# Modulation vectors of a two-layer transformer kernel: summed by VectorE among the projections, or multiplied by TensorE in the attention

## The reference

```python
def layer(x, ctx, c, c_ctx, w_mod, b_mod, ...):
    shift, scale, gate = jnp.split(jax.nn.silu(c) @ w_mod + b_mod, 3, axis=-1)
    shift_c, scale_c, gate_c = jnp.split(jax.nn.silu(c_ctx) @ w_mod + b_mod, 3, axis=-1)
    hx = rmsnorm(x, g_pre) * (1 + scale[:, None]) + shift[:, None]
    hc = rmsnorm(ctx, g_pre) * (1 + scale_c) + shift_c
    # projections q, k, v, ga, uf, gf, zc, bc, cc, gc = hx @ w_in (and the same of hc in layer 0)
    # window attention over own and context keys, a Fourier mix, a short convolution, a gated merge with w_out
    x_new = x + gate[:, None] * rmsnorm(y, g_post)
    ctx = ctx + gate_c * rmsnorm(yc, g_post)      # layer 0 only
```

## Time and profile before

| | us |
|---|---|
| median of 3 runs | 2080.86 |
| lowest, highest | 2075.86, 2082.39 |
| the profiled execution, whole | 2084.84 |
| its span (first to last instruction) | 2083.0 |
| first block, about | 760 |
| attention of layer 0, layer 1 | 132.5, 82 |
| projections of layer 0 after q1, layer 1 after q1 | 159, 110 |

### The profile page before, as it was taken

One profiled execution on the slowest core, in us unless ns is written; L12 is line 12 of the kernel. 1 busy time (PEld: TensorE's weight loads), 2 busy tenths in 40 slices (PEclk: granted clock), 3 DMA queues, 4 the chain that ended last, 5 costly groups with the idle time before them and its releaser, 6 DMA issues.

```text
span 2083.0 us, 27285 instructions
## 1 busy us (share of the span) xinstructions
PE 2012.9 (97%) x10646; PEld 1670.8 (80%) x10646; DVE 704.9 (34%) x1701; ACT 859.2 (41%) x1620; POOL 777.1 (37%) x616
## 2 busy tenths in 40 slices
PE   8999999999999999989999999999998999999997
PEld 4888888877888978867888888888877788888885
DVE  3121355343325445177431111017337551111004
ACT  3221377446237546477332222114557623222211
POOL 1433355315444134310344444434430144444442
PEclk9999989999999999999999999999989999999999
DMA  9521133221223123300233333222420123333320
GB/s 272 160 89 61 57 98 121 81 51 61 89 94 102 38 78 120 119 21 1 81 102 87 96 101 103 100 94 82 122 87 11 42 81 101 84 99 101 115 88 41
DMA packets 206310, 183.74 MB, mean 88 GB/s; under 512 B 31686, under 2 KB 182588, under 8 KB 206184
## 3 DMA queue, kind: packets, MB, share of 16 engines
q1 hardware_dynamic: 200152, 170.67, 27.2%
q10 hardware_dynamic: 6032, 11.33, 1.6%
HBM read 179.86 MB, written 5.40 MB: 89 GB/s over the span
## 4 chain that ended last, share of the span: by engine, by line
PE 85%; DVE 6%; ACT 4%; POOL 2%; issue 2%; DMA 0%; ACTq 0%; SPq 0%; DVEq 0%
PE ps L1263 22%; PE ps L1265 22%; PE ps L1264 22%; PE ps L1363 3%; PE ps L1856 3%; PE ps L1871 3%; POOL w_lo L691 2%; PE ps L1882 2%; PE ps L1337 2%; PE ps L1349 2%; PE ps L1301 1%; PE ps L1394 1%; ACT w_hi L745 1%; DVE sc L2429 1%; DVE sc L2441 1%
## 5 line engine op out<-in xcount | busy, mean ns | idle before, releaser
L691 POOL TENSOR_TENSOR w_lo<-raw,w_hi 128x512 fp32r<-128x512 f32 x582 | 755.2, 1329 | 1201.2 <-ACT w_hi L745 1201.1
L745 ACT ACTIVATE w_hi<-raw 128x1024 fp32r<-128x1024 f32 (+2 forms) x293 | 291.5, 1037 | 246.7 <-PE ps L1265 244.4
L1263 PE MATMUL ps<-g_hi,w_lo 128*128 128x512 f32 (+1 forms) x928 | 352.7, 380 | 1.6 <-POOL w_lo L691 1.6
L1264 PE MATMUL ps<-g_lo,w_hi 128*128 128x512 f32 (+1 forms) x928 | 351.8, 379 | 0.0
L1265 PE MATMUL ps<-g_hi,w_hi 128*128 128x512 f32 (+1 forms) x928 | 351.8, 379 | 0.0
L1263 PEld LDWEIGHTS ps<-g_hi,w_lo 128*128 128x128 f32 x928 | 174.6, 188 | 38.2 <-issue 1.3
L1265 PEld LDWEIGHTS ps<-g_hi,w_hi 128*128 128x128 f32 x928 | 174.6, 188 | 35.9
L1264 PEld LDWEIGHTS ps<-g_lo,w_hi 128*128 128x128 f32 x928 | 174.6, 188 | 35.2
L1263 PE MATMUL ps<-h_hi,w_lo 128*128 128x512 f32 (+1 forms) x496 | 181.0, 365 | 2.0 <-POOL w_lo L691 1.2
L1264 PE MATMUL ps<-h_lo,w_hi 128*128 128x512 f32 (+1 forms) x496 | 175.9, 355 | 0.0
L1265 PE MATMUL ps<-h_hi,w_hi 128*128 128x512 f32 (+1 forms) x496 | 175.8, 354 | 0.0
(11 more groups left out here) (282 smaller groups left out, 3451.0 us busy)
## 6 DMA issues: line engine op xcount, KB each, us to landing
raw<-in_w_in SPq DMA_DIRECT2D x30, 1024.0 KB, 5.3
raw<-in_w_mod SPq DMA_DIRECT2D x24, 1024.0 KB, 5.3
raw<-in_w_gate SPq DMA_DIRECT2D x44, 512.0 KB, 3.9
raw<-in_w_up SPq DMA_DIRECT2D x44, 512.0 KB, 5.2
raw<-in_w_down SPq DMA_DIRECT2D x22, 1024.0 KB, 4.8
raw<-in_w_out SPq DMA_DIRECT2D x8, 1024.0 KB, 5.1
strips<-bias_rows ACTq DMA_DIRECT2D x18, 256.0 KB, 4.1
raw<-in_w_in SPq DMA_DIRECT2D x16, 256.0 KB, 4.5
```

What stands on the lines that cost most here:

```text
L691: pool.tensor_tensor(w_lo[:, i % SPLIT, a:e], raw_of(what)[:, a:e], w_hi[:, i % SPLIT, a:e].bitcast(F32), ALU.subtract).then_inc(s_tile_lo ...
L745: act.activation(w_hi[:, i % SPLIT, a:b], raw_of(what)[:, a:b], ACT.Copy).then_inc(s_tile_hi.sem, s_tile_hi.nth((what, n)))
L1263: pe.matmul(o, lhs[1], rhs[0], start=first, stop=False)
L1264: pe.matmul(o, lhs[0], rhs[1], start=False, stop=False)
```

## The change

The sixteen tiles of `w_mod` are no longer split nor given to TensorE as moving data. They are cut into eight blocks of 512 columns (`BLOCKS`), each in two tiles of 4 x 128 rows (`WEIGHED`), and loaded among the projection tiles (`GOES_BEFORE`): two before kv, two before uf, one each before gf, zc, bc, two before cc, one before gc and two before ga0 in layer 0; one each before uf, gf, zc and cc in layer 1. VectorE's `weigh` multiplies each 128 x 512 piece of the raw tile by the condition value of its partition and adds it up in `acc` (float32, in SBUF), for both condition vectors: eight operations a tile, 128 in all. SyncE's load of a tile three places behind such a tile waits for its weigh. TensorE's `add_up` then sums the partitions of a block: eight matmuls with 128x128 pieces of `acc` as the stationary part and one column of ones, placed in a projection's PSUM bank before its part 1 (layer 0) or ahead of a projection (layer 1). VectorE's `summed_in` adds the bias. `mod`, `mod_fm`, `mod_out_row`, `mods_out` and `cond_hl` are gone, and so are the splits in the attention. The constants' and `w_fourier`'s loads now stand ahead of the first weighed tile instead of kv. The freed bank 7 gives the attention a second output bank (`slots`).

```diff
@@ stream
+        BLOCKS = [(0, 4), (0, 5), (1, 0), (1, 1), (1, 2), (1, 3), (1, 4), (1, 5)]
+        WEIGHED = [(l, "mod", jb, kh) for l, jb in BLOCKS for kh in range(2)]
+        GOES_BEFORE = {(0, "kv"): (0, 1), (0, "uf"): (2, 3), (0, "gf"): (4,), (0, "zc"): (5,), (0, "bc"): (6,), (0, "cc"): (7, 8),
+                       (0, "gc"): (9,), (0, "ga", 0): (10, 11), (1, "uf"): (12,), (1, "gf"): (13,), (1, "zc"): (14,), (1, "cc"): (15,)}
+        SUMMED = {(0, "kv", 1): 0, (0, "gf", 0): 1, (0, "zc", 0): 2, (0, "bc", 1): 3, (0, "gc", 0): 4, (0, "ga", 0, 1): 5,
+                  (1, "zc", 0): 6, (1, "ga", 0, 0): 7}
-            stream += mix + [mod_tile(*m) for m in mods_in_attention[l]] + outs
+            for tile in mix:
+                for m in GOES_BEFORE.get(tile[0], ()):
+                    wl, _, jb, kh = WEIGHED[m]
+                    stream.append((WEIGHED[m], [square(I["w_mod"][wl], jb, kh)], False))
+                stream.append(tile)
+            stream += outs
-        MOD_STEP = (4, 6)
-            return sc, pt, 1024, (2, 1, 1, 4)
+            return sc, pt, 1024, (2, 1, 2, 4)
@@ sync
+                    elif stream[n - RAW][0] in WEIGHED:
+                        sp.wait_ge(s_weigh.sem, s_weigh.at(stream[n - RAW][0]))
@@ scalar
+                    if j == 1:
+                        act.wait_ge(s_mod.sem, s_mod.at(("sum", 5 + 2 * l)))
-                    if step >= 4 and (step - 4) % MOD_STEP[l] == 0 and mods:
-                        mod_out_row(mods.pop(0))
-                        split_next((0,))
-                        halves.append(step)
-                    elif halves and step == halves[-1] + 2:
-                        halves.pop()
-                        split_next((1,))
@@ tensor
+            def add_up(n, b):
+                pe.wait_ge(s_weigh.sem, s_weigh.at(WEIGHED[2 * n + 1]))
+                for h in range(2):
+                    for c in range(4):
+                        o = 256 + 2 * c + h
+                        m = pe.matmul(ps[:, b, o:o + 1], acc[n % 2][h][:, P * c:P * c + P], ones[:, 0:1], start=True, stop=True)
+                m.then_inc(s_mod.sem, s_mod.nth(("sum", n)))
+                emptied[b] = s_mod_in.after(("sum", n))
-                        if before:
-                            mod_fm(before.pop())
-                        mod(what)
-                        before.append(what)
@@ vector
+            def weigh(m):
+                what, n, kh = WEIGHED[m], m // 2, m % 2
...
+                wait_landed(dve, what)
+                for k in range(4):
+                    for h in range(2):
+                        to, w = acc[n % 2][h], raw_of(what)[:, 512 * k:512 * k + 512]
+                        by = cond[:, 4 * kh + k, h:h + 1]
+                        if kh == 0 and k == 0:
+                            V.tensor_scalar(to[:], w, by, None, ALU.mult).then_inc(s_weigh.sem, s_weigh.nth((what, k, h)))
+                        else:
+                            dve.wait_ge(s_weigh.sem, s_weigh.at((what, k - 1, h) if k else (WEIGHED[m - 1], 3, h)))
+                            V.scalar_tensor_tensor(to[:], w, by, to[:], ALU.mult, ALU.add).then_inc(s_weigh.sem, s_weigh.nth((what, k, h)))
```

More of the change, by code:

```diff
@@ L220, in _program @@
         ao1 = at("ao1", [P, NT, 512], uf_at)
+        acc_at = names["ga"][0] + 2 * 4 * TOK
+        acc = [[at("acc00", [P, 512], acc_at), at("acc01", [P, 512], acc_at + 2048)],
+               [at("acc10", [P, 512], acc_at + 4096), at("acc11", [P, 512], names["mod_row"][0])]]
+        assert names["mod_row"][1] == 2048 and 6144 <= 2 * 4 * TOK
         tmp_m = at("tmp_m", [P, 2, 512], names["q1"][0])
@@ L472, in _program @@
         assert all(split_at[(DEPTH + l, "up")] % SPLIT == UP_SLOT for l in range(DEPTH))
-        mods_all = FIRST + [what for what, _, _ in stream if what[1] == "mod" and what not in FIRST]
-        mod_at = {what: i for i, what in enumerate(mods_all)}
         ROW_BANK = (4, 5, 6, 7, 2, 4, 5, 2)
@@ L969, in _ @@
                     split_next()
-                mods = [(m, "mod", j) for m, j in mods_in_attention[l]]
                 n_q = len(units1(l)) // HEADS
-                halves = []
                 def between(step):
@@ L1289, in paired @@
                 return [(0, 0), (1, 0), (0, 1), (1, 1), (2, 0), (3, 0), (2, 1), (3, 1)]
-            def mod(what):
-                i = mod_at[what]
-                o = ps[0:4, 7, 0:256]
-                w = both_parts(begin(what), lambda r: r.rearrange("p (k c) -> p k c", k=KD))
-                if i >= 1:
-                    pe.wait_ge(s_mod_row.sem, s_mod_row.at(mods_all[i - 1]))
-                for part in range(2):
-                    for k in range(KD):
-                        need(what, 256 * (k + 1))
-                        m = pe.matmul(o, cond_hl[:, k, :], w[1 - part][:, k, :], start=part == 0 and k == 0, stop=part == 1 and k == KD - 1)
-                m.then_inc(s_mm.sem, s_mm.nth(what))
-                left(what)
-            def mod_fm(what):
-                i = mod_at[what]
-                l, _, j = what
-                pe.wait_ge(s_mod_row.sem, s_mod_row.at(what))
-                for c in range(2):
-                    o = 256 + 64 * l + 2 * (2 * j + c)
-                    m = pe.matmul(ps[:, 7, o:o + 2], mod_row[0:4, i % 2, P * c:P * c + P], fold[0:4, :], start=True, stop=True)
-                m.then_inc(s_mod.sem, s_mod.nth(what))
+            def add_up(n, b):
[6 more added lines that the diff above has]
+                emptied[b] = s_mod_in.after(("sum", n))
             def attend(y, units, at_step):
@@ L1365, in attend @@
                     at_step(step)
-                for b in range(7):
+                for b in range(8):
                     if 512 * b < width * n_s:
@@ L1513, in fm @@
                         emptied[b] = until.after((l, what, c, part))
+                        if part == 1 and (l, *what, c) in SUMMED:
+                            add_up(SUMMED[l, *what, c], b)
                         for k in range(KD):
@@ L1589, in _ @@
                             n_rot += 1
+                        if l == 1 and (l, what, c) in SUMMED:
+                            pe.wait_ge(*emptied[4])
+                            add_up(SUMMED[l, what, c], 4)
                         fm((what,), c, w, s_conv_t if what == "cc" else s_proj)
@@ L1594, in _ @@
                     for c in range(2):
+                        if l == 1 and (l, "ga", j, c) in SUMMED:
+                            pe.wait_ge(*emptied[5])
+                            add_up(SUMMED[l, "ga", j, c], 5)
                         fm(("ga", j), c, w, s_proj)
@@ L1637, in _ @@
                 units = units1(l)
-                mods = [(m, "mod", j) for m, j in mods_in_attention[l]]
-                before = []
                 def between(step):
@@ L1643, in between @@
                         fourier(step)
-                    if step >= 3 and (step - 3) % MOD_STEP[l] == 0 and mods:
-                        if step == 3:
-                            pe.wait_ge(*emptied[7])
-                        what = mods.pop(0)
-                        if before:
-                            mod_fm(before.pop())
-                        mod(what)
-                        before.append(what)
-                attend(l, units, between)
-                while mods:
-                    what = mods.pop(0)
-                    mod_fm(before.pop())
-                    mod(what)
-                    before.append(what)
-                mod_fm(before.pop())
-                emptied[7] = s_mod_out.after((l, 1))
+                attend(l, units, between)
                 pe.wait_ge(s_lo.sem, s_lo.at((l, "s", SIDES[3])))
@@ L2170, in _ @@
                 if l == 0:
+                    weigh(0)
+                    weigh(1)
                     dve.wait_ge(s_consts.sem, 16 * len(consts))
@@ L2221, in _ @@
                 q_lo(1)
+                summed_in((5, 7)[l])
                 def k_lo_part(g):
```

91 lines of the change are left out of this document (58 added, 33 removed).

## The result

The changed kernel took 2028.6 us (median of 4 runs, 2018.2 to 2029.1) beside 2081.6 before (4 runs, 2075.9 to 2093.6): ratio 0.973, interval 0.967 to 0.978. The forecast was 2060 with a range of 2043 to 2079: the sign was right, and the gain of 53 us was two and a half times the 20.5 forecast. The profiled execution has a span of 2027.3 us (before 2083.0).

The account below looks back on a forecast made before the run. TensorE, busy 97% of the span, was taken as the bound. Gains 36.1 + 2.6 + 1 less costs 15.2 (add_up) and 4 (queue order) gave 20.5 us off the 2080.86 median: 2060 us, range 2043 to 2079.

Parts of the forecast that it names:

- cond_hl and the two mods_out go: Small removed VectorE and ScalarE work of 0.2 to 0.4 us beside a busy TensorE, forecast to gain nothing.
- rival C: Half-clock stretch in layer 0's attention is a chance event: 2052 if it stays away, 2068 if a second comes; chance 0.12.
- The matmuls: Removing the attentions' modulation tiles from TensorE: 2.37 us a tile at full clock, 36.1 us gained in all.
- ScalarE's share: Removing mod_row copies and splits ahead of attention's copies: +6.6 us of waits, net 2.6 after a charge of 4.
- the heads' ends: Charge in layer 0's attention for half-width context units: 0.5 us for each of eight heads, -4 us.
- The second bank: Second attention output bank lets a product start earlier: about 1 us in layer 0, 0.5 in layer 1; gain 1 booked.
- the first tile is no gain: Each attention's first modulation tile: TensorE waits for ScalarE's copy anyway, so 3.7 us in two layers turn into wait.
- Rival A: Attention stays coupled: waits open where modulation tiles filled gaps, costing 10 us in layer 0, 3 in layer 1; 2073; chance 0.14.
- add_up: Eight added summations on TensorE in the projections, fully on the path: 1.9 us each, cost 15.2, bounds 13.5 and 20.
- The two sizes: Sign of a right forecast: VectorE weigh operations near 0.75 us and, when meeting GpSimd, 1.67, mean near 1.0.
- Rival B: VectorE becomes the bound in layer 0 from 86 us and layer 1's rope: 38 us cost instead of 4, 2094; chance 0.08.
- Queue order: Raw-slot loads in the projections wait for weighs, delaying tiles and rotations: cost 4 us, bounds 0 and 12.

Follow-up runs that it names:

- e1: Changed kernel with 128 unused bytes per partition where cond_hl stood, undoing the layout shift; 2052.4 us, ratio 0.983.
- e2: Kernel before with 384 unused bytes per partition behind cond_hl, giving the changed kernel's layout within 512 bytes; 2055.7 us, ratio 0.986.
- e15: Changed kernel run again without any edit, on an earlier occasion than its other repeat; 2028.8 us, ratio 0.973.
- e8: Kernel before with one matmul instead of sixteen in each attention modulation tile, ScalarE's work kept; 2082.2 us, ratio 0.998.
- e6: Kernel before with a 128-byte tensor in front of all others in SBUF; 2083.4 us, ratio 1.001.
- e12: Changed kernel with one attention output bank and sixteen unread matmuls added at each of the sixteen old modulation steps; 2045.6 us, ratio 0.981.
- e9: Changed kernel with each add_up as one matmul of eight columns instead of eight of one column; 2006.8 us, ratio 0.962.
- e11: Changed kernel with each of the 128 VectorE weighing operations doubled; 2086.1 us, ratio 1.001.
- e10: Changed kernel with six of the eight VectorE weighing operations of each tile left out; 2024.3 us, ratio 0.970.
- e16: Changed kernel with twelve unread matmuls added behind the third and the fourth step of each attention; 2016.0 us, ratio 0.966.
- e4: Changed kernel with 256 unused bytes per partition behind cond; 2027.0 us, ratio 0.971.
- e7: Changed kernel with 64 unused bytes per partition behind cond; 2036.0 us.
- e13: Changed kernel with 192 unused bytes per partition behind cond; 2044.2 us.
- e14: Changed kernel with 32 unused bytes per partition behind cond; 2051.0 us.

## Why the prediction was wrong

**The step that failed most is one that it put at nothing.** "cond_hl and the two mods_out go: ... nothing" counted the work and not the place. 25 to 26 us of the 53 come from that line (e1, e2), in matmuls that the change doesn't touch. The prediction had no term for anything behind layer 1's attention.

**Clock.** The forecast recovered 1.9 us of clock, for one tile in one stretch, and called the stretch a chance event with rival C at 0.12. In the profiled pair the clock stayed 3.4 us better in layer 0 and 6.8 worse in the untouched rest, where profiles of one and the same kernel differ by more (15.2 in e15, 26.6 in after). "Chance" was wrong for the place of the stretch (17 profiles of 17) and right for its length. That other waits of 1.46 "brought none" was read rightly, but it didn't mean that they can't: one of three did in e8, with the modulation matmuls gone, and one of four in e6, with all of them in place.

**Attention.** Net of lost clock, layer 0 went from 123.1 to 91.2 us, 32, and the terms of the sum (30.8 with 1.9 of clock) give 28.9. That this comes so near is partly luck, for its parts were sized otherwise. The matmuls: 1.6 us a tile (e8, e12) instead of 1.84, 18 instead of 20 for eleven tiles. ScalarE's share: 6 to 7 us instead of the 1.3 that were left of 5.3 after 4 had been charged for the heads' ends; that charge was the mistake, with 1.73 us a unit measured against 1.71 + 0.08. The second bank: 3 to 4 instead of 1. That the first tile is no gain was right: from the first turned probabilities (277.51 in the changed kernel, 277.79 in e12) to the next ones (281.87, 282.16) it takes 4.36 us without the sixteen matmuls and 4.37 with them. Layer 1: 9.9 us, 9.5 forecast. Rival A is out: no coupling beyond 0.25 us a head.

**add_up.** 1.70 us each, 13.6 in all, 15.2 forecast; at the lower bound, and on the path (e9).

**VectorE.** A tile takes (88.1 + 10.1) / 16 = 6.1 us, forecast 6.2 alone and 9.9 where it meets GpSimd; the mean of an operation is 0.77 us of busy time, not the 1.0 that the prediction gave as its sign. The two sizes are there: 112 of the 128 took under 0.8 us and 15 between 1.4 and 1.80; a tile took 4.9 to 9.0. By the letter of the Trainium skill's rule ("SBUF — State Buffer", "Who interferes with whom") a tile that meets GpSimd would cost 11.2 us, an estimate; that the two exclude each other fits the two sizes of the earlier trace rows, but they met far less often than I took. Rival B stayed out; with twice the work it comes (e11).

**Queue order.** Charged with 4 us; nothing of it shows: e10 has the same order with a quarter of the weighing and gains under 1 us, TensorE waits 0.8 us in all in layer 0's projections, as before, and its only wait near a rotation of layer 1 is the 0.8 us for uf_lo that stood there before. From before to e1 (same layout) the projections and the middle grew by 8.1 + 3.4 = 11.5 us net of lost clock, where sum and order were to cost 19.2. Of the 7.7 us, 1.6 are add_up and 4 the order; 2 are not attributed.

In spans the miss is (2083.0 - 20.5) - 2027.3 = 35.2 us. Layout is 25.9 of it (e1 to after). The work is 12.9 (31.5 from before to e1, against 20.5 - 1.9): 7.7 the added work priced too high, 2.5 and 1.3 the attentions (from e1's stages, net of clock, so good to 2 or 3 us), and 1.4 are not attributed. The clock takes 3.6 back: 1.7 us more lost over the whole span, where 1.9 fewer were forecast.

## What to carry to other kernels

A tensor removed or added moves all that is allocated behind it: before you credit a change of a few per cent, read the pace of matmuls that it doesn't touch, and pad one of the two kernels until they stand alike. Where TensorE waits beside a slow partner, work that it does in between can keep its clock (e8, e16); price the removal of such work with the lost clock as a separate term, and compare kernels by stretches at full clock before you compare whole stages. A charge for trouble that no row shows, like the 4 us for the heads' ends, needs a row too. And a doubled or quartered load (e10, e11) tells in two runs on which side of the bound a hidden engine lies.

## What the runs showed of the hardware

- The pace of a 512-column float32 `mm3` matmul behind another depends on the distance in SBUF between moving and stationary operand: 226.7 ns in the changed kernel and with 256 bytes more, 232.5 with 128 more; 32 and 192 bytes more cost the same or a little more, 64 less (e1, e2, e4 to e7, e13, e14). Matmuls of 256 columns don't share it: 283 ns in the changed kernel, 282 with 128 bytes more, 278 to 279 with 32, 64 or 192.
- TensorE's clock fell to half for 58 us of an attention, in three stretches at waits of 1.76, 3.33 and 1.46 us (e8). It stayed at full behind a wait of 0.69 us where 24 matmuls had been added (e16), behind one of 1.70 in e12, and behind two more of 1.46 in e8.
- A half-clock stretch of 3.4 to 17.1 us stood at the first waits of layer 0's attention in 17 of 19 profiles; each us of lost clock there cost 0.7 us.
- A float32 matmul of one column with a new 128x128 stationary part costs 0.21 us (1.70 / 8) from start to start, two records of 0.106 each.
